# Memory queries from the un-normed sum, with two of their units between the scores of the first heads

## The reference

```python
x = layer_norm(ALPHA * x + hybrid_mixer(...), ln1_g, ln1_b)
x = layer_norm(ALPHA * x + memory_cross_attention(x, mem, xa_wq, xa_wkv, xa_wo), ln2_g, ln2_b)
def layer_norm(x, g, b):
    mu = x.mean(-1); var = square(x - mu).mean(-1)
    return (x - mu) * rsqrt(var + EPS) * g + b
def memory_cross_attention(x, mem, wq, wkv, wo):      # 4 heads of 256
    q = x @ wq
    p = softmax(q @ k.T / 16);  return (p @ v) @ wo
```

## Time and profile before

| | |
|---|---|
| times of three runs | 883.8, 886.33, 886.41 us |
| profiled execution | 886.01 us |
| its span | 884.2 us |
| mean granted clock of TensorE | 0.973 |
| PE, DVE, ACT busy | 852.1, 650.8, 482.7 us (96%, 74%, 55%) |

### The profile page before, as it was taken

The page is one execution under the profiler, slowest core; times in us unless marked ns, Lnnn a source line. Parts: engine busy times, 40 slices in busy tenths (PEclk is TensorE's granted clock), DMA queues, the critical chain, the costliest instruction groups (busy, mean ns, idle before and its releaser), DMA issues.

```text
span 884.2 us, 15825 instructions
## 1 busy us (share of the span) xinstructions
PE 852.1 (96%) x6396; PEld 805.5 (91%) x6396; DVE 650.8 (74%) x1011; ACT 482.7 (55%) x708; POOL 7.6 (1%) x17
## 2 busy tenths in 40 slices
PE   8999999999999999999997999999998999999997
PEld 7889987989889999999996999898998899999885
DVE  5787797767667888887867896787797866665553
ACT  5643456554547666655546636566547654444452
POOL 0200000000000000000000000000000000000000
PEclk9999999979988999999998999999998899999999
DMA  9986658837143765558852555475564376775751
GB/s 335 246 262 212 212 173 257 255 107 238 45 147 99 222 186 186 176 197 264 267 193 72 162 161 153 155 234 162 190 205 153 95 256 218 225 234 183 176 189 48
DMA packets 139592, 166.89 MB, mean 189 GB/s; under 512 B 5520, under 2 KB 123280, under 8 KB 139520
## 3 DMA queue, kind: packets, MB, share of 16 engines
q1 hardware_dynamic: 137712, 162.82, 58.4%
q0 software_dynamic: 720, 2.02, 1.2%
q10 hardware_dynamic: 1088, 1.05, 0.3%
HBM read 164.62 MB, written 1.25 MB: 188 GB/s over the span
## 4 chain that ended last, share of the span: by engine, by line
PE 62%; DVE 16%; ACT 6%; issue 3%; DVEq 0%; ACTq 0%
PE ps L520 61%; DVE lor L1612 6%; DVE FA L1612 3%; DVE FA L1615 2%; ACT hir L1105 2%; DVE FA L1618 1%; DVE raw L1629 1%; ACT FA L1298 0%; DVE FA L2295 0%; DVE X L1615 0%; ACT FA L1231 0%; DVE X L1612 0%; ACT FA L1491 0%; PE ps L762 0%; ACT L1120 0%
## 5 line engine op out<-in xcount | busy, mean ns | idle before, releaser
L1612 DVE TENSOR_TENSOR lor<-raw,hir 128x1024 fp32r<-128x1024 f32 (+1 forms) x267 | 309.7, 1177 | 108.0 <-ACT hir L1105 105.7
L1105 ACT ACTIVATE hir<-raw 128x1024 fp32r<-128x1024 f32 (+1 forms) x257 | 260.2, 1032 | 119.6 <-PE ps L520 111.5
L520 PE MATMUL ps<-INH,hir 128*128 128x256 f32 (+1 forms) x1064 | 306.7, 288 | 4.2 <-ACT INH L1273 2.5
L520 PE MATMUL ps<-INH,lor 128*128 128x256 f32 (+1 forms) x1064 | 302.5, 284 | 2.9 <-DVE lor L1612 2.9
L520 PE MATMUL ps<-INL,hir 128*128 128x256 f32 (+1 forms) x1064 | 302.9, 285 | 1.1 <-DVE INL L1612 0.9
L520 PEld LDWEIGHTS ps<-INH,hir 128*128 128x128 f32 x1064 | 204.6, 192 | 7.3 <-issue 5.8
L520 PEld LDWEIGHTS ps<-INH,lor 128*128 128x128 f32 x1064 | 204.3, 192 | 5.1 <-DVE lor L1612 4.0
L520 PEld LDWEIGHTS ps<-INL,hir 128*128 128x128 f32 x1064 | 203.8, 192 | 2.1 <-DVE INL L1612 2.0
L520 PE MATMUL ps<-HIH,hir 128*128 128x256 f32 x688 | 197.5, 287 | 0.0
L520 PE MATMUL ps<-HIH,lor 128*128 128x256 f32 x688 | 194.5, 283 | 0.8 <-DVE lor L1612 0.8
L520 PE MATMUL ps<-HIL,hir 128*128 128x256 f32 x688 | 193.8, 282 | 0.0
(11 more groups left out here) (271 smaller groups left out, 772.2 us busy)
## 6 DMA issues: line engine op xcount, KB each, us to landing
raw<-in_w_in SPq DMA_DIRECT2D x64, 512.0 KB, 4.6
raw<-in_mod_wT SPq DMA_DIRECT2D x48, 512.0 KB, 4.4
raw<-in_ffn_w_up SPq DMA_DIRECT2D x44, 512.0 KB, 4.5
raw<-in_w_ffn_in SPq DMA_DIRECT2D x44, 512.0 KB, 4.6
raw<-in_w_ffn_out SPq DMA_DIRECT2D x22, 512.0 KB, 4.6
raw<-in_ffn_w_down SPq DMA_DIRECT2D x20, 512.0 KB, 4.7
raw<-in_xa_wkv SPq DMA_DIRECT2D x16, 512.0 KB, 4.5
raw<-in_xa_wq SPq DMA_DIRECT2D x8, 512.0 KB, 4.9
```

The source lines that it names most:

```text
L520: return e.matmul(o, l, r, start=start, stop=stop, skip_group_check=True)
L1105: e.activation(hi, src, ACT.Copy).then_inc(*w_hi.up(i))
L1612: return e.tensor_tensor(o, a, b, op)
```

## The change

The norm no longer stands before the queries. After each unit of `w_out` ScalarE writes gain times `X` to `xg1` (in HIH) and VectorE its low half; two extra columns carry gain and bias. The four query units multiply that (`late_g`, 128x258, one half in a `lin` bank, the other in an `att` bank). xq0 and xq1 are cut into steps, between which the norm's sums and the two spreads stand. ScalarE copies the mean's and the deviation's row from PSUM to `st`. `settle(c)` makes the queries: per half VectorE copies two factors and does mean times factor minus product, then both halves times the deviation; ScalarE negates and adds the bias. xq2 runs in step 0 of the attention before `lx0`, xq3 in step 1 before `lx1`. `X` itself is normed in the attention loop, a quarter after each `put` (`normed` on VectorE, `affine` on ScalarE). The modulation chunks of the query units move to the down units.

```diff
-    add2(("xq", 0), A["xa_wq"], 0, ("xq", 1), A["xa_wq"], 256, mod=1)
+    add2(("xq", 0), A["xa_wq"], 0, ("xq", 1), A["xa_wq"], 256)
     for c in (2, 3):
-        add(("xq", c), A["xa_wq"], 256 * c, 8, mod=1)
+        add(("xq", c), A["xa_wq"], 256 * c, 8)
...
-        add(("down", c), A["ffn_w_down"], 256 * c, 22, mod=2 + c // 3, spread=True)
+        add(("down", c), A["ffn_w_down"], 256 * c, 22, mod=3, spread=True)
...
+        xg1 = Inp("xg1", HIHX[:, 0:8, :], HILX[:, 0:8, :])
...
-                w.wait_ge(act.at(("xg", "hi ext")), dve.at(("xg", "lo ext")))
+                w.wait_ge(act.at((x.name, "hi ext")), dve.at((x.name, "lo ext")))
...
+                if between:
+                    next(between)
...
+            mm.mark("xg1 free")
             for c in range(4):
                 unit(("wout", c), 8, mix)
-            mm.mark("x1 free")
-            layer_norm("n1")
             mm.mark("before cross attention")
-            run(units_g([("xq", 0), ("xq", 1)], 8, x1))
-            unit(("xq", 2), 8, x1)
-            unit(("xq", 3), 8, x1)
-            mm.mark("oc free")
+            g = late_g([("xq", 0), ("xq", 1)], xg1, 2)
+            steps_of(g, 1)
+            row_sums("n1", 3, X[:, 6:8, :], g)
+            steps_of(g, 1)
+            spread_bank(("n1", "mu"), SN[:, 0:2])
+            spread_bank(("n1", "r"), SN[:, 6:8])
+            run(g)
+            def query_done(*cs):
+                for c in cs:
+                    for j in range(2):
+                        (lin, att)[j].release(("unit", ("xq", c), j))
+            query_done(0, 1)
             for i in range(6):
+                if i < 2:
+                    run(late_g([("xq", 2 + i)], xg1, 2))
+                    query_done(2 + i)
+                if i == 1:
+                    mm.mark("oc free")
                 if i < 4:
                     b, before = att.get(("lx", i), bank)
-                    w.wait_ge(copied(before), dve.at(("QC", i)), act.at("KV"))
+                    w.wait_ge(copied(before), act.at(("QC", i)), act.at("KV"))
...
+            def gained(c):
+                for k in (2 * c, 2 * c + 1):
+                    w.wait_ge(dve.at(("n1", "x", c)), vec_in.at(0), mm.at("xg1 free"))
+                    e.activation(xg1.hi[:, k, 0:T], X[:, k, :], ACT.Copy, scale=V("ln1_g", k)).then_inc(*act.up(("xg1", "hi", k)))
+                if c == 0:
+                    for i, n in enumerate(("ln1_g", "ln1_b")):
+                        e.activation(xg1.hi[:, :, T + i:T + i + 1], V(n, n=8).unsqueeze(2), ACT.Copy).then_inc(*act.up(("xg1", "hi ext")))
+            def settle(c):
+                for j in range(2):
+                    w.wait_ge(dve.at((("xq", c), "normed")))
+                    e.activation(QC[:, 2 * c + j, :], QC[:, 2 * c + j, :], ACT.Identity, scale=-1.0, bias=GB2[c % 2][j][:, 1:2]).then_inc(
+                        *act.up(("QC", c)))
             for c in range(4):
                 ahead.unit(("wout", c), 8)
                 square("n1", c, X[:, 2 * c:2 * c + 2, :], dve.at(("n1", "x", c)), squares_free("n1", None, c))
+                gained(c)
                 if c == 2:
                     preload(ACT.Sqrt)
-            layer_norm("n1", "ln1_g", "ln1_b", x1, "x1 free")
             act.mark("before cross attention")
-            ahead.units([("xq", 0), ("xq", 1)], 8)
-            ahead.unit(("xq", 2), 8)
-            ahead.unit(("xq", 3), 8)
+            late = ahead.units_g([("xq", 0), ("xq", 1)], 8)
+            next(late)
+            w.wait_ge(dve.at(("n1", "var")))
+            e.activation(SN[:, 4:6], SN[:, 2:4], ACT.Sqrt).then_inc(*act.up(("n1", "deviation")))
+            w.wait_ge(mm.at(("n1", "mu")), mm.at(("n1", "early")))
+            e.activation(MB, bank["n1", "mu"][:, 0:T], ACT.Copy).then_inc(*act.up("mean row", ("out", ("n1", "mu"))))
+            run(late)
+            w.wait_ge(mm.at(("n1", "r")))
+            e.activation(RB, bank["n1", "r"][:, 0:T], ACT.Copy).then_inc(*act.up("deviation row", ("out", ("n1", "r"))))
+            ahead.more()
+            ahead.more()
+            settle(0)
+            settle(1)
+            def affine(c):
+                for k in (2 * c, 2 * c + 1):
+                    w.wait_ge(dve.at(("n1", "normed", c)))
+                    e.activation(X[:, k, :], X[:, k, :], ACT.Identity, scale=V("ln1_g", k), bias=V("ln1_b", k)).then_inc(
+                        *act.up(("n1", "affine")))
             for i in range(6):
+                if i < 2:
+                    ahead.unit(("xq", 2 + i), 8)
+                if i in (1, 2):
+                    settle(1 + i)
...
                     put(oc, 2 * h, 2, OCF[:, 2 * h:2 * h + 2, :])
+                    affine(h)
...
-                w.wait_ge(mm.at(("unit", (key, c))), x_in[3].at(0))
+                w.wait_ge(mm.at(("unit", (key, c))), x_in[3].at(0), *([act.at(("n1", "affine"))] if name == "n2" else []))
...
+            def gained(c):
+                for k in (2 * c, 2 * c + 1):
+                    w.wait_ge(act.at(("xg1", "hi", k)))
+                    stt(xg1.lo[:, k, 0:T], X[:, k, :], V("ln1_g", k), xg1.hi[:, k, 0:T].bitcast(F32), MUL, SUB).then_inc(
+                        *dve.up(("xg1", "lo", k)))
...
+            late = ahead.units_g([("xq", 0), ("xq", 1)], 8)
...
+            e.reciprocal(SN[:, 6:8], SN[:, 4:6]).then_inc(*dve.up((("n1", "r"), "factor")))
+            next(late)
+            def normed(c):
+                d = X[:, 2 * c:2 * c + 2, :]
+                w.wait_ge(act.at("mean row"), act.at(("xg1", "hi", 2 * c + 1)), dve.at(("xg1", "lo", 2 * c + 1)))
+                tt(d, d, over(MB, 2), SUB).then_inc(*dve.up())
+                w.wait_ge(act.at("deviation row"), dve.last())
+                tt(d, d, over(RB, 2), MUL).then_inc(*dve.up(("n1", "normed", c)))
+            def settle(c):
+                key, dst = ("xq", c), QC[:, 2 * c:2 * c + 2, :]
+                for j in range(2):
+                    b, vs = bank["unit", key, j], GB2[c % 2][j]
+                    w.wait_ge(mm.at(("unit", key, j)), *([act.at(("QC", c - 2))] if c >= 2 else []))
+                    e.tensor_copy(vs, b[:, T:T + 2]).then_inc(*dve.up())
+                    w.wait_ge(dve.last(), act.at("mean row"), *before)
+                    stt(dst[:, j, :], MB, vs[:, 0:1], b[:, 0:T], MUL, SUB).then_inc(*dve.up(("out", ("unit", key, j))))
+                w.wait_ge(dve.last(), act.at("deviation row"))
+                tt(dst, dst, over(RB, 2), MUL).then_inc(*dve.up((key, "normed")))
+            run(late)
+            ahead.more()
+            ahead.more()
+            settle(0)
+            settle(1)
             for i in range(6):
+                if i < 2:
+                    ahead.unit(("xq", 2 + i), 8)
...
+                    if i in (0, 1):
+                        settle(2 + i)
...
+                    normed(h)
```

More of the change, by code:

```diff
@@ L327 @@
 UNITS = ((0, 1), (1, 1), (2, 2), (4, 2), (6, 2))
+LATE = [("xq", c) for c in range(4)] + [("q", 2), ("k", 2)]
 def build(nc, A, out):
@@ L350, in build @@
         INH, INL = INHX[:, :, 0:T], INLX[:, :, 0:T]
-        HIH = sb("HIH", 22 * TE, F32R)[:, :].rearrange("p (k t) -> p k t", t=TE)[:, :, 0:T]
-        HIL = sb("HIL", 22 * TE, F32R)[:, :].rearrange("p (k t) -> p k t", t=TE)[:, :, 0:T]
+        HIHX = sb("HIH", 22 * TE, F32R)[:, :].rearrange("p (k t) -> p k t", t=TE)
+        HILX = sb("HIL", 22 * TE, F32R)[:, :].rearrange("p (k t) -> p k t", t=TE)
+        HIH, HIL = HIHX[:, :, 0:T], HILX[:, :, 0:T]
         SQ = sb("SQ", 1024)[:, :].rearrange("p (a n) -> p a n", a=2)
@@ L436, in build @@
         SN = SMALL[:, 424:436]
+        GB2 = [[SMALL[:, 436 + 4 * i + 2 * j:438 + 4 * i + 2 * j] for j in range(2)] for i in range(2)]
         SS, VP, VR4, SD4, RR = (CH[:, a:a + n] for a, n in ((0, 4), (4, 2), (6, 2), (8, 2), (10, 2)))
@@ L447, in build @@
         MS2 = C("mstrict").unsqueeze(1).to_broadcast([128, 2, 128])
-        xin, x1, x2, h2, mg, oc = (Inp(n, INH, INL) for n in ("xin", "x1", "x2", "h2", "mg", "oc"))
+        xin, x2, h2, mg, oc = (Inp(n, INH, INL) for n in ("xin", "x2", "h2", "mg", "oc"))
         xg = Inp("xg", INHX, INLX)
+        xg1 = Inp("xg1", HIHX[:, 0:8, :], HILX[:, 0:8, :])
         mem, hid, hd = (Inp(n, HIH, HIL) for n in ("mem", "hid", "hd"))
@@ L488, in last_matmul @@
                 return "read", i
-            return ("unit", key, 1) if kind == "wide" or key in (("q", 2), ("k", 2)) else ("unit", key)
+            return ("unit", key, 1) if kind == "wide" or key in LATE else ("unit", key)
         before_in_slot, seen = {}, {}
@@ L777, in tensor, with row_sums @@
             run(fill)
-            def row_sums(name, c, src):
+            def row_sums(name, c, src, between=None):
                 b, before = att.get((name, "sums"), bank)
@@ L1921, in layer_norm @@
                 tail(*pend)
+            def gained(c):
[3 more added lines that the diff above has]
+                        *dve.up(("xg1", "lo", k)))
+                if c == 0:
```

(28 more changed lines are left out.)

## The result

The changed kernel takes 893.38 us (median of 8, 890.89 to 896.83) against 886.35 (8 runs beside it, 883.8 to 891.25). The ratio is 1.0085, interval 1.0061 to 1.0108: slower by 7.0 us. The forecast was 891.9, inside what the interval leaves open (891.8 to 895.9). The profiled execution is the longest of the eight, 896.83. It holds two stretches of half clock under a busy TensorE, at 121 and 462 us, that the profile of before doesn't have; a third is in both, at 618 us before and 630 after (more on them at the end).

The account below looks back on a forecast made before the run. TensorE bounds the kernel (62% of the chain), so only its waits or lower clock can be won. The terms -5.7 + 3.9 + 1.7 + 4.4 + 0.4 + 1.2 = +5.9 on 886.01 give 891.9 us, range 888 to 896.

Parts of the forecast that it names:

- A: Norm under the first two query units: xq2 can start at 197.8 instead of 203.5, -5.7 us.
- B: Three products into xq2, its second half waits for a bank until head 0 is settled: +3.9 us, bounds 2.5 and 4.5.
- C: Behind xq2's bank wait, 3.4 us of work at half clock: +1.7 us, between 0 and 2.85.
- D: Attention: new waits of 1.8 before px1, 3.1 before px3, 2.9 before ox3, less 3.4 old: +4.4 us.
- E: Half clock behind the attention's two waits over 2.0 us, on 1 to 2 us of work each: +1.2, between 0 and 3.4.
- the 5 below which the prediction called itself wrong: Sign in attention: waits before px1, px3 and ox3 together below 5 us would show the prediction wrong.
- The 0.4: First xo unit finds the oc halves of the last head late: +0.4 us.
- the terms at nothing: Edits costed at 0: modulation chunks moved to the down units (if not, +0.7), and the second norm's waits for `affine`.
- SQ, the sums and the residual of the second norm wait for `affine`: Second norm: these wait for `affine`, which ends before the first xo unit does, so cost 0.
- The down units' spare time of VectorE: Down units: VectorE at 13.41 of 15.00; the moved chunks' further 1.2 per 15.7 us leaves 0.4 or more.
- the faster one: Attention: xq3's 5.7 us gives VectorE time to clear `settle(2)` and the normed sums, clock holds; -3.0, 883.0 us; chance 0.08.
- The stall in A: Second query unit's first weights come late on ScalarE: 1.1 us, bounds 0 to 2.5; the skill's drain rule adds 1.4.

Follow-up runs that it names:

- the first experiment: Changed kernel with head 0's query settled ahead of the low halves of xq3's weights instead of behind them: 887.19 us, ratio 1.0003.
- the early norm: Changed kernel with quarters 0 and 1 of X normed behind head 1's settling, 2 and 3 behind the split in step 0: 887.28 us, ratio 1.0003.
- the chunks back: Changed kernel with the three modulation chunks back in the query units from the down units: 893.27 us, ratio 1.0071.
- the later table load: Changed kernel with the square root's table loaded behind the split after the last square, not behind the third square: 893.13 us, ratio 1.0063.
- all queries first: Changed kernel with all four query units and their settling ahead of the attention: 897.52 us, ratio 1.0123.

## Why the prediction was right, and where it was not

**A** held: -5.4 for -5.7. The stall is 0.82 for 1.1, the 128x258 products take 0.121 each and not 0.118. The 5.5 us "of idle time and own products" that the prediction gives the norm is the busy part alone (5.46 in the earlier trace rows); the stretch is 7.46 long. The sum for A doesn't use it.

**B** held in size, place and cause (3.98; the first experiment took it away by VectorE's order alone).

**C**, "the clock after that wait", held in kind. Its size differs between executions: a loss of 1.5 us in the profiles of the early norm, the chunks back and the later table load, of 3.0 in the changed kernel's own and in that of all queries first. The forecast of 1.7 is near the first size; the profiled execution of the changed kernel, its longest, has the second.

**D** held in its waits: 1.44 for 1.8, 2.70 for 3.1, and ox3's 2.60 for 2.9 where the clock was full. Its sum has a slip. It takes 3.4 us of old waits off the new ones, as what is left of 18.8 us beside the products, but the earlier trace rows show waits of 2.7 (and the earlier trace rows 18.53 us busy of 21.20). By its own waits D was +5.1 and the whole forecast 892.6. In the profile of the chunks back the waits are 6.7 less 2.7, so 4.0, the half clock costs 1.6 more, and D and E together come to 5.7 for 5.6: the waits forecast too long and the slip cancel, which is luck.

**E** held there, too. In the changed kernel's own profile the half clock lies over px3 and ox2 while ScalarE prepares what ox3 waits for, so the wait shrinks to 1.06 and the two cover one another: 4.2, not 5.6. By this the three waits come to 5.2, just above the 5 below which the prediction called itself wrong.

**The 0.4 and the terms at nothing.** The +0.4 for late oc halves at the first xo unit did not come. "SQ, the sums and the residual of the second norm wait for `affine`, which ends before the first xo unit does: 0" named the right order and missed what is queued on ScalarE behind the last `affine`: two splits, behind whose low halves the first residual stands. The wait for the last residual is 1.82 after and 0.51 before, and 0.95 where half clock lies over xo's first products; the stage costs 1.5 in the changed kernel's profile and 0.5 and 0.7 in the other two, where the forecast had 0. The down units' spare time of VectorE was there, but ScalarE waits 10.5 us for weights that the DMA brings, and TensorE 1.0. In the medians this is 0 to 2 and not settled.

So the mechanism is the forecast one, and the 1.5 us between 891.9 and 893.38 is within what the interval leaves open. In the longest execution C and the second norm are larger and E smaller; in the two nearer the median C, D and E come as forecast, and the second norm is the only stage that clearly was missing. Of the rivals, the faster one (xq3 gives VectorE the time) failed where the prediction said, at `normed(0)` behind the values of head 0; the run with all queries first shows that its first half was true, the interleaving is worth 3 to 4 us. The stall in A as the Trainium skill's page "ScalarE: Activation LUTs" ("What ACT_TABLE_LOAD costs") would have it, 1.4 longer by a drain, did not come: in the changed kernel the load starts 0.01 behind the last gain copy and the next ACTIVATE 1.30 later.

```profile
179.95 0.90 ACT L1303 ACTIVATE HIH<-X,vec 128x256 fp32r<-128x256 f32 x2
180.86 1.28 ACT L1138 ACT_TABLE_LOAD   x1
182.16 0.20 ACT L1138 ACTIVATE small<-con 1x1 f32<-1x1 f32 x1
```

## What to carry to other kernels

Taking a norm off TensorE's path won its 5.4 us, and two pieces of vector work in the wrong place, the settling of head 0 and the norming of `X`, cost some 6 us each: when products are moved ahead of a vector chain, look at each bank's last reader and what is queued in front of it, and put work that nothing waits for yet (here the norming of `X`) into an idle stretch and not between a head's scores and its weights. A wait and the half clock behind it may cover the next wait, so don't add them without asking what else is late then. And where two fixes win 6 us each, measure both together before adding them: here they won less than 2 us more than one, where 6 were expected. One profile is one execution: where a stage has two sizes, as the half clock behind xq2's wait has, lay several profiles beside one another before calling a term too small.

## What was not expected of the hardware

TensorE's clock falls to 0.50 for 3 to 4 us also where TensorE is kept busy, at a price of 1.5 to 1.7 us each (121.0 to 124.5 and 462.5 to 465.5 above). From 450.0 to 462.5 us TensorE had been busy for 12.50 of 12.50 us. The stretch at 121 starts 2.3 us behind the end of a wait of 0.82, but the kernel before has that wait as well (0.81) and no half clock behind it. They come in some executions and not in others, at the same stages in different kernels: near 12, 54, 121, 452 to 465 and 618 to 633 us, none to three of them in each of 14 profiles. The loss by half clock is between 12.3 and 20.5 us of an execution, and the scatter of the times goes with the clock: of 88 timed runs of the kernel before, the 15 with a mean granted clock of 0.977 or more have a median of 884.7 us, and the 10 with 0.970 or less one of 888.6. Why these stretches come, and whether the total is steered by something, no run here settles.
